# Gates by joined products, a fifth place for split weights at the second norm, and a first unit split by halves, in a two-block float32 kernel

## The chip, the core and the metric

The kernel runs on one core of a Trainium2 chip. The metric is the time of one execution on the device in microseconds (us); several executions are timed and their median is given. TensorE is called PE here (PEld for its weight loads), VectorE DVE, ScalarE ACT, GpSimd POOL and SyncE SP, as in the profile.

## The reference

Two residual blocks run one after the other over 256 tokens of width 1024 in float32. The first has a Mamba-2 mixer and an RG-LRU mixer, joined by gates, and a gated feed-forward block (FFN). The second has four branches, each gated and projected up, then summed and projected out:

```python
def _layer(x, mem, ...):
    h = _rmsnorm(x, norm_pre)
    cols = h @ w_in
    (dn_qkv, dn_z, dn_b, dn_a, gm_uv, gm_z, sw_q, sw_k, sw_v, sw_z,
     xm_q, xm_z, gate_logits) = _split_cols(cols)
    mem_kv = _rmsnorm(mem, norm_mem) @ w_mem_kv
    y_a = _deltanet_branch(dn_qkv, dn_z, ...)      # o * silu(z), z = dn_z
    y_b = _spatial_gating_branch(gm_uv, gm_z, ...)
    y_c = _sliding_window_branch(sw_q, sw_k, sw_v, sw_z, sinks)   # o * silu(z), z = sw_z
    y_m = _memory_branch(xm_q, xm_z, mem_kv)
    proj = jnp.einsum("btnc,ncd->btnd", ys, w_up)
    merged = jnp.sum(sigmoid(gate_logits) * proj, axis=2)
    return x + _rmsnorm(merged @ w_out, norm_post)
```

The change is about `sw_z` and `dn_z` (512 columns each), about the norms between the FFN and this block, and about the very first product.

## The kernel before

**Weights in units.** All weights come from one stream of 258 units of 128x1024 float32 (512 KB). SP fetches them in order into five buffers `t_raw`, each fetch behind the split of the unit five before it. A unit is split in two: ACT writes its high part to `t_wh` (fp32r), then DVE writes the rest, raw minus high, to `t_wl` (`split`, L1333 on ACT and L1903 on DVE). There are NS = 4 places for split units, so unit q's place is free when PE has finished unit q-4. PE waits for the low part before it starts a unit.

**Products.** Inputs are split too, into Hh and Hl, two halves of one tile `t_hx`. A product is high by high, high by low and low by high; low by low is left out. In `three` (L643 to L645) this takes three matmuls with 256 columns (tokens) for each 128 rows of weights; a unit has eight such k steps, a chunk of 256 output columns has two units, and its two halves lie in one PSUM bank. `chunk_apart` (L701), used by 19 of the 24 FFN chunks, joins the first two: one matmul of 512 columns multiplies the high weights by Hh and Hl together, and one of 256 adds the low weights by Hh to one half:

```python
mm(two(b), wh[:, k, :], HX[:, :, k, :], k == 0, False)
return mm(half(b, 1), wl[:, k, :], Hh[:, k, :], False, k == 7)
```

Each unit then fills a bank, and DVE adds the bank's halves with a TENSOR_REDUCE (L2613). `turned` (L728) makes rows of tokens: the inputs are stationary, the weights move in 512 columns, and token tiles tt = 0 and 1 go to two banks, six matmuls each per unit.

**Order.** Each engine's program is written out in one fixed order. A counter is advanced after each unit (`tick`, and `mid` inside a unit on PE) and at set counts lets the lanes go on: delta rule (`dn`), memory attention (`xm`), sliding attention (`sw`) and others. So an engine does unit work, then what its lanes have due, then the gate of the chunk, strictly in that order. Three banks, 0 to 2, go round among the chunks; who had a bank before (`bank_table`, L263, and `evacuated`, L532) must have been read before PE writes it again.

**Gates.** `swz0`, `swz1`, `dnz0`, `dnz1` are the last chunks before the gate logits `gt3_0`. Each is 2 units. When a chunk is done ACT takes tanh(z/2) from the bank (`half_tanh`, L1807), and DVE computes (tanh + 1) * z (`gated`, L2631) from the bank again.

**The second norm** (`second_norm`, L1389 on ACT, L2034 on DVE) stands between the FFN and the second block: squares of the FFN's output, its norm, the residual, the norm of the sum, the scaled rows; then PE transposes them (`turn_tile`, L772), tile by tile, and ACT and DVE take high and low parts. While it runs PE has four units of its own: `mk2` (two) and `mk3` (two), from the memory's normed rows, of which the last comes after the first transposes. After them `vu` (four units) needs the transposed rows. `walk.ahead(n)` inside the norm splits units up to n at set places among the norm's steps.

**The start.** ACT scales the input's high parts, then splits unit 0, takes squares and splits unit 1; DVE follows with the low parts. PE has the small product for dt, then `xbc4` with unit 0, in whose second unit it sums the squares (`mix_sums`); in `xbc5` it spreads the row of the norm over all partitions (`norm_spread`), and DVE and ACT make the normed inputs from that.

Of the kernel before, what the change touches and what calls it, by code (L numbers as in the profile page):

```python
# [202 lines left out]
class Walk:  # L203
# [5 lines left out]
    def unit(self, ahead=NS - 1):  # L209
        q = self.q  # L210
        self.q += 1
        while self.split_to <= min(q + ahead, NU - 1):
            self.split(self.split_to)
            self.split_to += 1
        return q

    def ahead(self, q):
        while self.split_to <= q:
            self.split(self.split_to)
            self.split_to += 1  # L220
# [124 lines left out]
def build_program(nc, first, gates, ws, par, con, masks, bd, rows, swt, xin, xtok, min_, post, decay, gates2, out):  # L345
    ctx = ExitStack()
    with ctx:
# [47 lines left out]
        s_raw = [sem(f"s_raw{i}") for i in range(NR)]  # L395
        HX = sb("hx", [P, 2, 8, T], R)
# [43 lines left out]
        FSUM = ar(32, 4, T)  # L440
        QKV = ar(0, 12, T)
# [90 lines left out]
        def evacuated(name):  # L532
# [106 lines left out]
        def pe_program(e):  # L639
# [13 lines left out]
            def weights(q, a):  # L653
                return [w[q % NS][:, :].rearrange("p (a b) -> p a b", a=a) for w in (WH, WL)]

            def split_ready(q):
                e.wait_ge(*lo.of(q))
# [507 lines left out]
            chunk("xbc4", YBh, YBl, {(1, 4): mix_sums})  # L1165
# [85 lines left out]
            for i in range(2):  # L1251
                for j in range(2):
# [47 lines left out]
            for name in ("swz0", "swz1", "dnz0", "dnz1"):  # L1300
                chunk(name, Hh, Hl)
# [30 lines left out]
        def act_program(e):  # L1332
            def split(q):  # L1333
                e.wait_ge(s_raw[q % NR], 16 * (q // NR + 1))
                if q >= NS:
                    e.wait_ge(*unit_done(q - NS))
                e.activation(WH[q % NS][:, :], RAW[q % NR][:, :], ACT.Copy, bias=0.0, scale=1.0).then_inc(*hi.now(q))  # L1337
# [51 lines left out]
            def second_norm(q):  # L1389
# [6 lines left out]
                walk.ahead(q + 1)  # L1396
# [22 lines left out]
                tile_parts(1, range(8))  # L1419
                act(BAS[:, :, 0:8], BAW, ACT.Copy).then_inc(*a_rw.now("w"))  # L1420
# [248 lines left out]
            split(0)  # L1669
# [106 lines left out]
            walk.four(3)  # L1776
# [30 lines left out]
            def half_tanh(name, dst):  # L1807
                for i in range(2):
                    walk.cols(f"{name}{i}")
                    chunk_done(f"{name}{i}")  # L1810
                    act(dst[:, 2 * i:2 * i + 2, :], two(BANK[f"{name}{i}"]), ACT.Tanh, scale=0.5).then_inc(*a_ev.now("tanh", f"{name}{i}"))
# [90 lines left out]
        def dve_program(e):  # L1902
            def split(q):  # L1903
                e.wait_ge(*hi.of(q))
                e.tensor_tensor(WL[q % NS][:, :], RAW[q % NR][:, :], WH[q % NS][:, :].bitcast(F), SUB).then_inc(*lo.now(q))  # L1905
# [128 lines left out]
            def second_norm(q):  # L2034
# [7 lines left out]
                walk.ahead(q + 1)  # L2042
# [6 lines left out]
                walk.ahead(q + 2)  # L2049
# [3 lines left out]
                walk.ahead(q + 3)  # L2053
                row_rsqrt(pre, 1, 1)
                scaled(pre, 1)
                walk.ahead(q + 4)
                tile_lows(0, range(6))
                walk.ahead(q + 5)
# [430 lines left out]
            split(0)  # L2489
# [128 lines left out]
            walk.four(3)  # L2618
            second_norm(FIRST["mk2"])
# [301 lines left out]
```

## Time and profile before

| | us |
|---|---|
| median of 3 runs | 853.13 (852.63 to 854.49) |
| the profiled execution: its own time | 853.44 |
| its span, first to last instruction | 851.6 |
| PE busy | 836.5 (98%), 5422 matmuls |
| DVE busy | 651.1 (76%) |
| ACT busy | 508.6 (60%) |
| POOL busy | 74.7 (9%) |
| DMA, share of 16 engines | 50.8% |

The share of busy time says how full an engine was. The timeline gives start and duration of each instruction, or of several alike merged (x2), and in brackets how long the engine was idle before it and which engine's instruction ended that. Matmul ends are modelled and overlap, so PE's pace is read from start to start.

### The profile page before, as it was taken

Reading aid. Unit: us, or ns where it says so; the run is one execution under the profiler, and the core shown is the slowest. Engines: PE = TensorE matmul, PEld = TensorE weight load, DVE = VectorE, ACT = ScalarE, POOL = GpSimd, SP = SyncE. Lnnn points to the kernel's source line nnn. Section 1 sums busy time; section 2 is a strip of 40 time slices with the busy share of each in tenths; the row PEclk is TensorE's granted clock in tenths of the full one; section 3 lists DMA queues with packets and bytes.
Section 4 is the critical chain, followed back from the end, with each engine's and each line's share of the span. In section 5 each row is a group of like instructions: output and inputs, shape, how many; then the busy total and the mean of one; then the engine's idle time right before and its main releaser. Section 6 shows DMA issues by size and latency. Waiting matters only on the chain. (4 is left out here: it accounts for less than half of the span.)

```text
span 851.6 us, 13942 instructions
## 1 busy us (share of the span) xinstructions
PE 836.5 (98%) x5422; PEld 754.9 (89%) x5422; DVE 651.1 (76%) x1169; ACT 508.6 (60%) x839; POOL 74.7 (9%) x76
## 2 busy tenths in 40 slices
PE   8999999999999999999999899999999999999996
PEld 6999999999989988888888699899899888888885
DVE  6887987998877877888777968788855476776765
ACT  6575778665377755565656878754554444545443
POOL 0100002001020211111111200140000020000000
PEclk9999999999999999999999999999999999999999
DMA  8657443467455655556555465644433332355641
GB/s 311 233 170 282 152 146 125 149 199 296 145 179 182 228 185 198 178 174 205 187 193 179 133 214 171 239 162 149 138 110 103 115 130 99 128 198 194 198 149 49
DMA packets 40585, 148.42 MB, mean 174 GB/s; under 512 B 4652, under 2 KB 5320, under 8 KB 39880
## 3 DMA queue, kind: packets, MB, share of 16 engines
q1 hardware_dynamic: 40520, 147.54, 50.8%
q8 instruction: 43, 0.70, 0.3%
q14 instruction: 22, 0.18, 0.1%
HBM read 146.44 MB, written 1.08 MB: 173 GB/s over the span
## 5 line engine op out<-in xcount | busy, mean ns | idle before, releaser
L1905 DVE TENSOR_TENSOR t_wl<-t_raw,t_wh 128x1024 fp32r<-128x1024 f32 x258 | 315.3, 1231 | 81.4 <-ACT t_wh L1337 80.0
L1337 ACT ACTIVATE t_wh<-t_raw 128x1024 fp32r<-128x1024 f32 x258 | 270.4, 1055 | 90.1 <-PE bank L648 49.9
L643 PE MATMUL bank<-t_hx,t_wh 128*128 128x256 f32 x832 | 241.9, 291 | 1.3 <-DVE t_wl L1905 1.2
L645 PE MATMUL bank<-t_hx,t_wl 128*128 128x256 f32 x832 | 235.4, 283 | 0.0
L644 PE MATMUL bank<-t_hx,t_wh 128*128 128x256 f32 x832 | 235.3, 283 | 0.0
L643 PEld LDWEIGHTS bank<-t_hx,t_wh 128*128 128x128 f32 x832 | 159.2, 191 | 4.0 <-DVE t_wl L1905 2.0
L644 PEld LDWEIGHTS bank<-t_hx,t_wh 128*128 128x128 f32 x832 | 159.2, 191 | 0.5
L645 PEld LDWEIGHTS bank<-t_hx,t_wl 128*128 128x128 f32 x832 | 159.1, 191 | 0.0
L648 PE MATMUL bank<-t_wh,t_hx 128*128 128x512 f32 x448 | 150.3, 401 | 3.2 <-DVE t_wl L1905 3.2
L648 PE MATMUL bank<-t_wh,t_br 128*128 128x512 f32 x384 | 123.5, 393 | 0.0
L648 PE MATMUL bank<-t_hx,t_wh 128*128 128x512 f32 x304 | 107.7, 398 | 0.0
L648 PEld LDWEIGHTS bank<-t_wh,t_hx 128*128 128x128 f32 x448 | 84.2, 188 | 20.9 <-DVE t_wl L1905 4.1
L648 PE MATMUL bank<-t_wl,t_hx 128*128 128x512 f32 x224 | 87.4, 390 | 0.0
L648 PEld LDWEIGHTS bank<-t_wh,t_br 128*128 128x128 f32 x384 | 72.1, 188 | 15.4 <-issue 0.2
L648 PE MATMUL bank<-t_hx,t_wl 128*128 128x256 f32 x304 | 85.3, 281 | 0.0
L648 PE MATMUL bank<-t_wl,t_br 128*128 128x512 f32 x192 | 74.9, 390 | 0.0
L1342 ACT ACTIVATE t_arena<-bank 128x512 f32<-128x512 f32 (+5 forms) x76 | 42.0, 573 | 54.4 <-PE bank L648 28.2
L648 PEld LDWEIGHTS bank<-t_hx,t_wh 128*128 128x128 f32 x304 | 57.1, 188 | 14.1
L2704 POOL TENSOR_TENSOR t_br<-t_arena,t_br 128x256 fp32r<-128x256 f32 x29 | 33.6, 1163 | 400.3 <-ACT t_br L1342 400.3
L648 PE MATMUL bank<-t_arena 128*128 128x128 f32 (+4 forms) x370 | 58.4, 305 | 1.2 <-DVE t_arena L2483 1.2
L648 PEld LDWEIGHTS bank<-t_hx,t_wl 128*128 128x128 f32 x304 | 57.4, 189 | 0.4
L1920 DVE SCALAR_TENSOR_TENSOR t_arena<-bank,t_par,t_arena 128x255 f32<-128x255 f32 (+3 forms) x108 | 43.9, 474 | 15.4 <-ACT t_arena L1342 15.0
(153 smaller groups left out, 984.4 us busy)
## 6 DMA issues: line engine op xcount, KB each, us to landing
t_raw<-in_ws SPq DMA_DIRECT2D x258, 512.0 KB, 4.0
t_br<-decay SPq DMA_DIRECT2D x1, 2048.0 KB, 8.8
t_arena<-in_post SPq DMA_DIRECT2D x3, 512.0 KB, 5.1
t_arena<-gates SPq DMA_DIRECT2D x1, 1536.0 KB, 10.4
t_x<-in_xin SPq DMA_DIRECT2D x2, 512.0 KB, 4.8
t_bd<-in_bd SPq DMA_DIRECT2D x1, 1024.0 KB, 7.5
t_x<-in_xtok SPq DMA_DIRECT2D x1, 1024.0 KB, 6.4
t_arena<-in_mem SPq DMA_DIRECT2D x1, 1024.0 KB, 8.5
```

The source lines that it names most:

```text
L643: e.matmul(o, wh, xh, start=first, stop=False, skip_group_check=True)
L644: e.matmul(o, wh, xl, start=False, stop=False, skip_group_check=True)
L645: return e.matmul(o, wl, xh, start=False, stop=last, skip_group_check=True)
L648: return e.matmul(o, l, r, start=st, stop=sp, skip_group_check=True)
L1337: e.activation(WH[q % NS][:, :], RAW[q % NR][:, :], ACT.Copy, bias=0.0, scale=1.0).then_inc(*hi.now(q))
L1342: return e.activation(o, i, f, bias=bias, scale=scale)
L1905: e.tensor_tensor(WL[q % NS][:, :], RAW[q % NR][:, :], WH[q % NS][:, :].bitcast(F), SUB).then_inc(*lo.now(q))
L1920: return e.scalar_tensor_tensor(out=o, in0=a, scalar=s, in1=b, op0=op0, op1=op1)
L2704: return e.tensor_tensor(o, a, b, op)
```

## The change

Four edits, with what goes with them:

1. `swz0`, `swz1`, `dnz0`, `dnz1` go through `chunk_apart`. Each unit has a bank of its own, DVE adds the halves of both banks to a new tile ZSUM (arena, float32), and tanh on ACT and the gate on DVE read ZSUM. The bank is free again at the event ("sum", chunk), when both units' halves are added.
2. The unit SPARE, the second of `mk2`, gets a place of its own in `t_br`, whose first half is idle there. It is split at the end of the FFN; inside the second norm `walk.ahead` passes over it, so each place where a unit was split now splits the one after it.
3. In `mk3`'s last unit PE does token tile 0, then `turn_tile(0)`, then token tile 1; before, `turn_tile(0)` came ahead of both.
4. Unit 0 is split in two halves of 512 columns on ACT and DVE, and PE waits for the second ahead of k step 4.

```diff
     def ahead(self, q):
         while self.split_to <= q:
-            self.split(self.split_to)
+            if self.split_to != SPARE:
+                self.split(self.split_to)
             self.split_to += 1
...
+SPARE = FIRST["mk2"] + 1
+def place(q):
+    return (q - (q > SPARE)) % NS
+def had_place(q):
+    if q == SPARE:
+        return LAST["fd9"]
+    return q - NS - (SPARE < q <= SPARE + NS)
+GATES_APART = ("swz0", "swz1", "dnz0", "dnz1")
...
+        elif name in GATES_APART:
+            for i in range(2):
+                n = (n + 1) % 3
+                bank[name, i] = n
...
             def split_ready(q):
-                e.wait_ge(*lo.of(q))
+                e.wait_ge(*(lo.of(q) if q else lo.of(0, "first")))
...
-            chunk("xbc4", YBh, YBl, {(1, 4): mix_sums})
+            chunk("xbc4", YBh, YBl, {(0, 4): lambda: e.wait_ge(*lo.of(0)), (1, 4): mix_sums})
...
-                    if i == 1 and j == 1:
-                        turn_tile(0)
                     for tt in range(2):
                         m = turned(f"mk{2 + i}", u, 4 * i + 2 * j, Hh, Hl, i == 0 and j == 0, i == 1 and j == 1, (tt,))
                         if i == 1 and j == 1 and tt == 0:
                             m.then_inc(*p_tok.now("mk3"))
+                            turn_tile(0)
...
-            for name in ("swz0", "swz1", "dnz0", "dnz1"):
-                chunk(name, Hh, Hl)
+            for name in GATES_APART:
+                chunk_apart(name)
...
+            def split_by_halves(q):
+                e.wait_ge(s_raw[q], 16)
+                for c in range(2):
+                    e.activation(WH[q][:, halves(c)], RAW[q][:, halves(c)], ACT.Copy, bias=0.0,
+                                 scale=1.0).then_inc(*(hi.now(q) if c else hi.now(q, "first")))
...
-                walk.ahead(q + 1)
+                walk.ahead(q + 2)
                 post_squares(post, 1, 0)
...
-                walk.ahead(q + 2)
+                walk.ahead(q + 3)
                 x_squares(post, pre, 1, 0)
                 x_squares(post, pre, 1, 1)
-                walk.ahead(q + 3)
+                walk.ahead(q + 4)
                 scaled(pre, 0)
                 root(pre, 1, 1)
-                walk.ahead(q + 4)
+                walk.ahead(q + 5)
                 scaled(pre, 1)
...
+                    if f"{name}{i}" in GATES_APART:
+                        e.wait_ge(*d_ev.of("sum", f"{name}{i}"))
+                        src = ZSUM
...
             def gated(name, dst):
+                if name in GATES_APART:
+                    at = GATES_APART.index(name)
+                    e.wait_ge(*(d_ev.of(GATES_APART[at - 1]) if at else d_gm.of("v", 1)))
+                    for i in range(2):
+                        e.wait_ge(*unit.of(FIRST[name] + i))
+                        m = e.tensor_reduce(ZSUM[:, i, :], two(BANK[name, i]).rearrange("p w t -> p t w"), AX.X, ADD)
+                    m.then_inc(*d_ev.now("sum", name))
                 e.wait_ge(*a_ev.of("tanh", name))
-                stt(dst, dst, 1.0, two(BANK[name]), ADD, MUL).then_inc(*d_ev.now(name))
+                stt(dst, dst, 1.0, ZSUM if name in GATES_APART else two(BANK[name]), ADD, MUL).then_inc(*d_ev.now(name))
```

**How it moves the order.** DVE at the end of `dnz1`, before: the split of a unit (TENSOR_TENSOR to `t_wl`), the maxima of the last memory-attention head (bank 7), its reciprocal and scaling (`t_px`), the gate of `dnz1` from bank 0, the next split.

```order
L1905 TENSOR_TENSOR t_wl0<-t_raw4,t_wh0 128x1024 [waits s_split_hi]
L2425 TENSOR_REDUCE t_sm<-bank7 128x1 [waits s_xm_pe]
L2425 TENSOR_REDUCE t_sm<-bank7 128x1
L1916 TENSOR_SCALAR t_sm<-t_sm 128x2 [waits s_xm_dve]
L2430 RECIPROCAL t_sm<-t_sm 128x2 [waits s_xm_act]
L1916 TENSOR_SCALAR t_px<-t_px,t_sm 128x256 [waits s_xm_dve]
L1916 TENSOR_SCALAR t_px<-t_px,t_sm 128x256
L1920 SCALAR_TENSOR_TENSOR t_arena<-t_arena,bank0 128x512 [waits s_evac_act]
L1905 TENSOR_TENSOR t_wl1<-t_raw0,t_wh1 128x1024 [waits s_split_hi]
```

The same place now, with `dnz1` in banks 0 and 1:

```order
L1951 TENSOR_TENSOR t_wl3<-t_raw4,t_wh3 128x1024 [waits s_split_hi]
L2477 TENSOR_REDUCE t_sm<-bank7 128x1 [waits s_xm_pe]
L2477 TENSOR_REDUCE t_sm<-bank7 128x1
L1968 TENSOR_SCALAR t_sm<-t_sm 128x2 [waits s_xm_dve]
L2482 RECIPROCAL t_sm<-t_sm 128x2 [waits s_xm_act]
L1968 TENSOR_SCALAR t_px<-t_px,t_sm 128x256 [waits s_xm_dve]
L1968 TENSOR_SCALAR t_px<-t_px,t_sm 128x256
L2690 TENSOR_REDUCE t_arena<-bank0 128x256 [waits s_unit,s_evac_dve]
L2690 TENSOR_REDUCE t_arena<-bank1 128x256 [waits s_unit]
L1972 SCALAR_TENSOR_TENSOR t_arena<-t_arena 128x512 [waits s_evac_act]
L1951 TENSOR_TENSOR t_wl0<-t_raw0,t_wh0 128x1024 [waits s_split_hi]
```

Two sums of halves have come in between the scaling and the gate, and the gate no longer reads a bank.

PE after `dnz1`, before: the scores of the last memory-attention head (bank 7), then the first unit of `gt3_0`, token tile 0 in bank 1 and token tile 1 in bank 2.

```order
L648 MATMUL bank7<-t_arena 128x256 [waits s_xm_dve]
L648 MATMUL bank7<-t_arena 128x256
L648 MATMUL bank1<-t_wh2,t_hx 128x512 [waits s_evac_dve,s_split_lo]
L648 MATMUL bank1<-t_wl2,t_hx 128x512
L648 MATMUL bank1<-t_wh2,t_hx 128x512 x2
L648 MATMUL bank1<-t_wl2,t_hx 128x512
L648 MATMUL bank1<-t_wh2,t_hx 128x512
L648 MATMUL bank2<-t_wh2,t_hx 128x512 [waits s_evac_dve]
L648 MATMUL bank2<-t_wl2,t_hx 128x512
L648 MATMUL bank2<-t_wh2,t_hx 128x512 x2
```

The same place now:

```order
L677 MATMUL bank7<-t_arena 128x256 [waits s_xm_dve]
L677 MATMUL bank7<-t_arena 128x256
L677 MATMUL bank2<-t_wh1,t_hx 128x512 [waits s_evac_dve,s_split_lo]
L677 MATMUL bank2<-t_wl1,t_hx 128x512
L677 MATMUL bank2<-t_wh1,t_hx 128x512 x2
L677 MATMUL bank2<-t_wl1,t_hx 128x512
L677 MATMUL bank2<-t_wh1,t_hx 128x512
L677 MATMUL bank0<-t_wh1,t_hx 128x512 [waits s_evac_dve]
L677 MATMUL bank0<-t_wl1,t_hx 128x512
L677 MATMUL bank0<-t_wh1,t_hx 128x512 x2
```

The tiles have moved to banks 2 and 0. Bank 0 was that of `dnz1`'s first unit, so the wait on `s_evac_dve` at the third row from the end is for the two sums above.

ACT in the second norm, before (`t_wh` rows are splits; `t_raw3` holds `mk2`'s second unit, `t_raw4` and `t_raw0` the two of `mk3`).

```order
L1342 ACTIVATE t_sm<-t_sm 128x1 [waits s_row_square,s_row_added]
L1337 ACTIVATE t_wh1<-t_raw3 128x1024 [waits s_unit,s_raw3]
L1363 ACTIVATE t_arena,t_sm<-bank6 128x512 [waits s_tokens_done]
L1363 ACTIVATE t_arena,t_sm<-t_x 128x512 [waits s_row_added]
L1363 ACTIVATE t_arena,t_sm<-bank7 128x512 [waits s_unit]
L1342 ACTIVATE t_sm<-t_sm 128x1 [waits s_row_square,s_row_added]
L1363 ACTIVATE t_arena,t_sm<-t_x 128x512 [waits s_row_added]
L1342 ACTIVATE t_sm<-t_sm 128x1 [waits s_row_square,s_row_added]
L1337 ACTIVATE t_wh2<-t_raw4 128x1024 [waits s_unit,s_raw4]
L1363 ACTIVATE t_arena,t_sm<-t_x 128x512 [waits s_row_added] x2
L1337 ACTIVATE t_wh3<-t_raw0 128x1024 [waits s_unit,s_raw0]
```

The same place now:

```order
L1376 ACTIVATE t_sm<-t_sm 128x1 [waits s_row_square,s_row_added]
L1365 ACTIVATE t_wh1<-t_raw4 128x1024 [waits s_unit,s_raw4]
L1397 ACTIVATE t_arena,t_sm<-bank6 128x512 [waits s_tokens_done]
L1397 ACTIVATE t_arena,t_sm<-t_x 128x512 [waits s_row_added]
L1397 ACTIVATE t_arena,t_sm<-bank7 128x512 [waits s_unit]
L1376 ACTIVATE t_sm<-t_sm 128x1 [waits s_row_square,s_row_added]
L1397 ACTIVATE t_arena,t_sm<-t_x 128x512 [waits s_row_added]
L1376 ACTIVATE t_sm<-t_sm 128x1 [waits s_row_square,s_row_added]
L1365 ACTIVATE t_wh2<-t_raw0 128x1024 [waits s_unit,s_raw0]
L1397 ACTIVATE t_arena,t_sm<-t_x 128x512 [waits s_row_added] x2
L1365 ACTIVATE t_wh3<-t_raw1 128x1024 [waits s_unit,s_raw1]
```

`t_raw3` is gone from the norm (it is split ahead of it, into `t_br`), and each split is of the unit after the one that stood there. DVE's order of splits moves in the same way.

## Rows read from the trace of the kernel before

**Rows 1.** Busy time by stretch: span, PE, PEld, DVE, ACT, POOL busy, PEclk, DMA share, GB/s
```profile
475.00:480.00 5.00, 3.01 (x12) 2.18 (x12) 4.89 (x12) 3.82 (x10) 0.00 (x0) 1.00 0.30 105
613.80:653.70 39.90, 39.80 (x332) 39.21 (x329) 22.84 (x34) 19.32 (x33) 0.00 (x0) 1.00 0.32 108
```

**Rows 2.** PE timeline, start: start us, us, instruction [idle before <-what ended it]
```profile
11.18 0.38 PE L643 MATMUL bank<-t_br,t_wh 128*128 128x256 f32 x1 [1.26 <-DVE t_wl L1905]
...
15.58 0.50 PE L648 MATMUL bank<-t_con,t_arena 128*128 128x1 f32 x4
```

**Rows 3.** PE timeline, second norm: mk2's second unit, mk3's first, turning, vu
```profile
475.50 0.50 PE L648 MATMUL bank<-t_wh,t_hx 128*128 128x512 f32 x1 [1.59 <-DVE t_wl L1905]
...
480.16 0.50 PE L648 MATMUL bank<-t_wh,t_hx 128*128 128x512 f32 x1 [1.65 <-DVE t_wl L1905]
...
483.05 1.04 PE L651 MATMUL bank<-t_con,t_arena 128*128 128x128 f32 x8
...
487.49 0.48 PE L648 MATMUL bank<-t_wh,t_hx 128*128 128x512 f32 x1
```

**Rows 4.** DVE timeline, start of the kernel
```profile
6.15 3.28 DVE L1920 SCALAR_TENSOR_TENSOR t_br<-t_x,t_arena,t_br 128x256 fp32r<-128x256 f32 x8 [2.92 <-ACT t_br L1342]
...
11.04 0.69 DVE L1910 TENSOR_TENSOR t_arena<-t_arena 128x512 f32<-128x512 f32 x1
...
13.03 1.94 DVE L1910 TENSOR_TENSOR t_arena<-t_arena 128x512 f32<-128x512 f32 x3
```

**Rows 5.** ACT timeline, start: split of unit 0; first normed input
```profile
8.82 1.04 ACT L1337 ACTIVATE t_wh<-t_raw 128x1024 fp32r<-128x1024 f32 x1
...
20.06 0.81 ACT L1342 ACTIVATE t_hx<-t_arena 128x256 fp32r<-128x256 f32 x2 [0.43 <-DVE t_arena L1920]
```

**Rows 6.** DVE timeline, second norm: three splits, then low parts of tile 0
```profile
469.46 1.23 DVE L1905 TENSOR_TENSOR t_wl<-t_raw,t_wh 128x1024 fp32r<-128x1024 f32 x1 [4.12 <-ACT t_wh L1337]
...
474.23 1.21 DVE L1905 TENSOR_TENSOR t_wl<-t_raw,t_wh 128x1024 fp32r<-128x1024 f32 x1
...
478.88 1.22 DVE L1905 TENSOR_TENSOR t_wl<-t_raw,t_wh 128x1024 fp32r<-128x1024 f32 x1
...
485.30 1.65 DVE L1920 SCALAR_TENSOR_TENSOR t_hx<-bank,t_par,t_hx 128x128 fp32r<-128x128 f32 x6 [0.32 <-ACT t_hx L1342]
```

**Rows 7.** ACT timeline, end of FFN, then scaled rows of either tile
```profile
464.46 0.42 ACT L1342 ACTIVATE t_br<-t_arena 128x256 fp32r<-128x256 f32 x1 [1.44 <-DVE t_arena L1910]
...
480.89 0.73 ACT L1342 ACTIVATE t_arena<-t_x,t_sm 128x512 f32<-128x512 f32 x1 [0.22 <-DVE t_sm L1917]
...
483.36 0.72 ACT L1342 ACTIVATE t_arena<-t_x,t_sm 128x512 f32<-128x512 f32 x1 [0.61 <-DVE t_sm L1917]
```

**Rows 8.** PE timeline, joined products, first and last of 32 k steps
```profile
398.28 0.39 PE L648 MATMUL bank<-t_hx,t_wh 128*128 128x512 f32 x1
...
409.57 0.40 PE L648 MATMUL bank<-t_wh,t_br 128*128 128x512 f32 x1
```

**Rows 9.** PE timeline, plain products of a chunk, 70 matmuls apart
```profile
562.80 0.28 PE L644 MATMUL bank<-t_hx,t_wh 128*128 128x256 f32 x1
...
571.20 0.28 PE L645 MATMUL bank<-t_hx,t_wl 128*128 128x256 f32 x1
```

**Rows 10.** DVE timeline, a pair of half sums in the FFN
```profile
443.81 1.28 DVE L2613 TENSOR_REDUCE t_arena<-bank 128x256 f32<-128x512 f32 x2
```

**Rows 11.** DVE timeline, the lane's last step and swz0's gate
```profile
627.34 1.01 DVE L1920 SCALAR_TENSOR_TENSOR t_arena<-t_arena,bank 128x256 f32<-128x256 f32 x2
```

**Rows 12.** ACT timeline, in swz1: the delta rule's bank is emptied
```profile
628.78 0.60 ACT L1342 ACTIVATE t_arena<-bank 128x512 f32<-128x512 f32 x1 [4.44 <-PE bank L648]
```

**Rows 13.** PE timeline: that bank's transposes; first matmul of gt3_0
```profile
630.82 0.60 PE L651 MATMUL bank<-t_con,t_arena 128*128 128x128 f32 x4
...
653.70 0.59 PE L648 MATMUL bank<-t_wh,t_hx 128*128 128x512 f32 x1
```

**Rows 14.** DVE timeline, end of dnz1: the gate, behind the memory lane's scaling
```profile
656.87 0.68 DVE L1920 SCALAR_TENSOR_TENSOR t_arena<-t_arena,bank 128x512 f32<-128x512 f32 x1
```

More of the change, by code:

```diff
@@ L211, in unit @@
         self.q += 1
[L212 to L214 removed]
+        self.ahead(min(q + ahead, NU - 1))
         return q
@@ L395, in build_program, with high, low @@
         s_raw = [sem(f"s_raw{i}") for i in range(NR)]
+        def high(q):
+            return BR[:, 0, 0:1024] if q == SPARE else WH[place(q)][:, :]
+        def low(q):
+            return BR[:, 1, 0:1024] if q == SPARE else WL[place(q)][:, :]
         HX = sb("hx", [P, 2, 8, T], R)
@@ L540, in evacuated @@
                     return d_ev.of(name[0])
+                if name[0] in GATES_APART:
+                    return d_ev.of("sum", name[0])
                 if name[0][:2] == "wo":
@@ L653, in weights @@
             def weights(q, a):
-                return [w[q % NS][:, :].rearrange("p (a b) -> p a b", a=a) for w in (WH, WL)]
+                return [w.rearrange("p (a b) -> p a b", a=a) for w in (high(q), low(q))]
             def split_ready(q):
-                e.wait_ge(*lo.of(q))
+                e.wait_ge(*(lo.of(q) if q else lo.of(0, "first")))
             def bank_free(name):
@@ L1335, in split @@
                 if q >= NS:
-                    e.wait_ge(*unit_done(q - NS))
-                e.activation(WH[q % NS][:, :], RAW[q % NR][:, :], ACT.Copy, bias=0.0, scale=1.0).then_inc(*hi.now(q))
+                    e.wait_ge(*unit_done(had_place(q)))
+                e.activation(high(q), RAW[q % NR][:, :], ACT.Copy, bias=0.0, scale=1.0).then_inc(*hi.now(q))
+            def split_by_halves(q):
[3 more added lines that the diff above has]
+                                 scale=1.0).then_inc(*(hi.now(q) if c else hi.now(q, "first")))
             walk = Walk(split)
@@ L1419, in second_norm @@
                 tile_parts(1, range(8))
+                e.wait_ge(*unit.of(SPARE))
                 act(BAS[:, :, 0:8], BAW, ACT.Copy).then_inc(*a_rw.now("w"))
@@ L1668, in act_program @@
                 act(YBh[:, k, :], X[:, k, :], ACT.Copy, scale=WMIX[:, k:k + 1]).then_inc(*a_xw.now(k))
-            split(0)
+            split_by_halves(0)
             for i in range(4):
@@ L1775, in act_program @@
                     walk.cols(f"fd{(j - 3) // 2}")
-            walk.four(3)
+            for j in range(4):
+                walk.unit(3 - j)
+            while walk.t < T_FU[23] + 1:
+                walk.tick()
+            split(SPARE)
+            while walk.t < T_FU[23] + 3:
+                walk.tick()
             chunk_done("fu23")
@@ L1809, in half_tanh @@
                     walk.cols(f"{name}{i}")
-                    chunk_done(f"{name}{i}")
-                    act(dst[:, 2 * i:2 * i + 2, :], two(BANK[f"{name}{i}"]), ACT.Tanh, scale=0.5).then_inc(*a_ev.now("tanh", f"{name}{i}"))
+                    if f"{name}{i}" in GATES_APART:
+                        e.wait_ge(*d_ev.of("sum", f"{name}{i}"))
+                        src = ZSUM
+                    else:
+                        chunk_done(f"{name}{i}")
+                        src = two(BANK[f"{name}{i}"])
+                    act(dst[:, 2 * i:2 * i + 2, :], src, ACT.Tanh, scale=0.5).then_inc(*a_ev.now("tanh", f"{name}{i}"))
             def rows_of_tokens(name, dst, f, event, scale=1.0):
@@ L1904, in split, with split_by_halves @@
                 e.wait_ge(*hi.of(q))
-                e.tensor_tensor(WL[q % NS][:, :], RAW[q % NR][:, :], WH[q % NS][:, :].bitcast(F), SUB).then_inc(*lo.now(q))
+                e.tensor_tensor(low(q), RAW[q % NR][:, :], high(q).bitcast(F), SUB).then_inc(*lo.now(q))
+            def split_by_halves(q):
+                for c in range(2):
+                    e.wait_ge(*(hi.of(q) if c else hi.of(q, "first")))
+                    e.tensor_tensor(WL[q][:, halves(c)], RAW[q][:, halves(c)], WH[q][:, halves(c)].bitcast(F),
+                                    SUB).then_inc(*(lo.now(q) if c else lo.now(q, "first")))
             walk = Walk(split)
@@ L2041, in second_norm @@
                 post_added(post, 0)
-                walk.ahead(q + 1)
+                walk.ahead(q + 2)
                 row_bias(post, 0, 1)
@@ L2048, in second_norm @@
                 post_added(post, 1)
-                walk.ahead(q + 2)
+                walk.ahead(q + 3)
                 row_rsqrt(pre, 1, 0)
@@ L2618, in dve_program @@
             walk.four(3)
+            split(SPARE)
             second_norm(FIRST["mk2"])
```

10 lines of the change are left out of this document (5 added, 5 removed).

## The prediction

> **What bounds the kernel now.** The table of busy time comes first: PE 98%, DVE 76%, ACT 60%, DMA 51% of the span. That is a mean over stages, so the windows are read next. In the 39.90 us that hold the four gates PE is busy for 39.80 and DVE for 22.84; in the 5 us around the second norm PE is busy for only 3.01 and DVE for 4.89 [rows 1]. So PE's stream sets the time, except where PE waits, and an edit is worth what it does to that stream. The brackets of PE's timeline give the waits that this change can touch, all ended by a low part from DVE: 1.26 us ahead of the first product [rows 2], 1.59 ahead of `mk2`'s second unit and 1.65 ahead of `mk3`'s first [rows 3]. They sum to 4.50 us; all else must come from PE doing less, or go by new waits.
>
> **Unit 0 by halves (edit 4).** ACT splits the whole unit from 8.82, for 1.04 [rows 5]; half of it is ready at about 9.39. DVE is held by the eight low parts of the input until 6.15 + 3.28 = 9.43, and a subtraction of 512 columns takes it 0.69 [rows 4]; so the first low half is there at about 10.15 and PE starts near 10.2, not 11.18: 1.0 earlier. It doesn't keep that. The sum of squares at 15.58 [rows 2] needs DVE's last additions, which end at 13.03 + 1.94 = 14.97 [rows 4], and some 0.1 later now, since two short splits cost more than a long one. So it comes near 15.1, and 0.48 is left. Then the norm's result releases ACT for the first normed input at 20.06, after an idle time of 0.43 [rows 5]: ACT is busy with splits until 19.63, so it can't begin before about 19.70. What is left is 0.36. **Term: −0.36**, ends 0 and −1.0.
>
> **The spare unit and the turning (edits 2 and 3).** Both waits of [rows 3] are for a split late in DVE's order [rows 6]. Now `mk2`'s second unit is split at the end of the FFN. ACT has 1.44 idle there [rows 7] for a split of 1.04, and DVE 4.12 [rows 6] for one of 1.2. So PE goes on without the wait of 1.59. The low part that ended at 474.23 + 1.21 = 475.44 [rows 6] is now that of `mk3`'s first unit, in time too; the one that ended at 478.88 + 1.22 = 480.10 is that of its second, and PE starts that unit at 480.16, where it started the first before. From there PE took 7.33 to `vu` (487.49 [rows 3]) for two units and two turnings. A unit is the 2.89 from 480.16 to the first turning at 483.05 [rows 3], a token tile 1.45 and a turning 0.78. Now: tile 0 to 481.61; the turning waits for ACT's scaled row, which ends at 480.89 + 0.73 = 481.62 [rows 7], and is done at 482.43; tile 1 to 483.88; the second turning waits for the scaled row that ends at 483.36 + 0.72 = 484.08 [rows 7] and is done near 484.95. `vu` needs its first two low parts: six take 1.65 from 485.30, a start that ACT's high parts set [rows 6], so two are there at 485.85, and `vu` starts near 485.95 instead of 487.49. Of the 3.24 removed, 1.70 comes back as three shorter waits. **Term: −1.54**. The ends are 0 (the order on ACT or DVE gives it all back) and −3.24.
>
> **Fewer matmuls in the gates (edit 1).** In the FFN 32 joined k steps take 409.57 − 398.28 = 11.29, or 0.3528 each [rows 8]. In a plain chunk 70 matmuls take 571.20 − 562.80 = 8.40, so 0.1200 each and 0.3600 a k step [rows 9]. The columns are the same 768, and only a fixed cost of one matmul falls away. Four chunks of 16 k steps: 64 × 0.0072 = 0.46. **Term: −0.46**. The Trainium skill, "TensorE: Matmul & The Clock Gate", section "Wait — 56ns, not 53.3ns?", has a fixed cost of about 2.5 ns a matmul beyond its columns at 2.4 GHz; by it 64 matmuls fewer give only 0.16, and the sum would end 0.30 higher. The trace's rows are used since they time these very forms.
>
> **The sums that this needs (edit 1).** DVE gains a pair of half sums per gate, 1.28 each time [rows 10], 5.1 in all. DVE has 17 us idle in that stretch [rows 1], so the work itself is covered; what isn't is work queued behind it, at two places.
>
> *At `swz0`.* The tanh on ACT used to wait for the product alone; now it waits for DVE, whose memory lane has a step before the gate ([rows 11]: two merged, the gate is the second, so the lane ends near 627.70). The sums end near 627.70 + 1.28 = 628.98, the tanh (0.6) near 629.5, then a split (1.04) near 630.5, and only then does ACT empty the delta rule's bank, which began at 628.78 after 4.44 idle before [rows 12]; it ends near 631.1. PE wants to transpose from it at 630.82 [rows 13], or some 0.1 earlier with joined products. **Term: +0.40**, ends 0 and +1.0. The next chunk's second unit wants the bank of the same sums near 629.1, which they just meet. At `swz1` and `dnz0` I take nothing, since DVE's idle time covers the shift; C below is the price if that cover is gone.
>
> *At the end of `dnz1`.* This is the largest term. `gt3_0` starts at 653.70 with token tile 0 [rows 13]. Its six matmuls take 1.45 as above, and 0.13 more behind the lane (the first lasts 0.59 here, 0.50 at 480.16), so tile 1 is due near 655.28. Its bank is now that of `dnz1`'s first unit, free when the sums are done. On DVE these stand behind the whole softmax of the last memory head. The gate followed the scaling at 656.87 [rows 14]; the sums take its place, and end at 656.87 + 1.28 = 658.15. The gate itself never held PE, since its bank wasn't wanted that soon. PE waits from 655.28 to about 658.25, that is 2.97, and its first matmuls after a wait cost 0.1 more, as at 475.50 (0.50, where the joined ones of [rows 8] last 0.39). Nothing behind gives it back: PE's stream simply goes on 3 us later. **Term: +3.07**. The ends are +2.0 (DVE reaches the softmax sooner) and +3.5 (the split and the maxima ahead of it shifted by 0.4).
>
> **Sum:** −0.36 − 1.54 − 0.46 + 0.40 + 3.07 = +1.11. The profiled execution took 853.44, which gives 854.55. It stood 0.31 above the median of the runs, so on the scale of that median it is 853.13 + 1.11 = **854.2**.
>
> **Rivals.**
> *A. The stall at `gt3_0` is absent or nearly so.* For it: DVE has 17 us idle in the stretch, and the softmax's wait for ACT may shrink. Against it: the order rows place both sums behind the scaling, without exception, and that scaling ends 1.6 us after the bank is wanted. Time: 853.13 + 1.11 − 3.07 = 851.2. Chance 0.15.
> *B. The second norm gives its gain back.* Its place is ACT and DVE at 463 to 486: if the spare's split finds its raw data or `t_br` late, ACT's high part of the last FFN input (464.46 [rows 7]) slips; DVE is nearly full there (4.89 of 5.00 [rows 1]). It decides once that slip is above the 1.54. Time: 854.2 + 1.54 = 855.8. Chance 0.11.
> *C. More of the order slips in the gates.* Tanh now waits for DVE four times, splits and bank emptying follow it on ACT. If PE waits at each of the three other gates as at `swz0`, or half a us each, it is +1.5: 855.7. Chance 0.08.
> *D. The clock falls in the wait of 3 us.* In [rows 1] the granted clock is 1.00, the 2.4 GHz level, through waits of 1.59 and 1.65. This one is almost twice as long, and no row here shows such a wait, or the 1.2 GHz level, in steady work. Bounds: nothing, as in those rows, and the wait's length again (3 us of products at half the clock take 6); taken in the middle, +1.5: 855.7. Chance 0.04. The Trainium skill, same page, section "HAM oscillation — how this bites in real kernels", describes such a fall of the clock after longer idle gaps of TensorE; where it applied, the time would be this rival's.
>
> **How the numbers follow.** The forecast has the remaining 0.62. A measurement of this kernel tells a change from none at about 0.2%, or 1.7 us: below 851.4 is faster, above 854.8 slower. The forecast is 0.6 below that upper bound, and its terms are loose by about 0.6 to one side (stall up to +3.5, `swz0` up to +1.0, the norm less than 1.54), so 0.45 of it falls within, 0.15 above and 0.02 below. A: two thirds of its 0.15 below 851.4. B, C and D (0.23) lie above but for 0.03. Together faster 0.12, same 0.53, slower 0.35. The forecast's own range is 853.3 to 855.2; the range of 8 in 10 reaches into A (851.6) and to B, C and D (856.2).
>
> **What the profile after would show.** PE's first product near 10.2, but the first normed input near 19.7. No PE wait at `mk2`'s second unit, about a us at `mk3`'s second, and short ones at the turnings and `vu`, which starts 1.5 earlier against the FFN's end. Gates with k steps of 0.353. In `gt3_0` a PE wait of about 3 us, ended by a TENSOR_REDUCE of DVE. The forecast is wrong if that wait is under 2 us, if the gates' k steps stay at 0.360, if `vu` doesn't start earlier against the FFN's end, or if PE waits over 1 us anywhere between `swz0` and `dnz1`.

## The result, and the profile after

The changed kernel takes 855.52 us in the median (12 executions, 853.79 to 855.74), against 853.13: a ratio of 1.0017 (95% interval 1.0009 to 1.0025), or 1.4 us slower. The two medians lie 2.4 apart, more than the ratio says, because the times fall into two groups, and the median before lies in the lower one, the median after in the upper one. The median is inside the predicted range of 8 in 10 (851.6 to 856.2) and 1.3 above the point of 854.2, but outside the forecast's own range (853.3 to 855.2): it lies in the part that was there for the rivals B, C and D. The profiled execution took 855.68, its span is 853.8. It stands against 853.44 and 851.6 before, so the two traces differ by 2.2 us.

The times of both kernels fall into these groups, some 1.5 us apart. Before: 8 of 12 in 852.63 to 853.57, 4 in 854.28 to 854.49. After: 4 of 12 in 853.79 to 854.13, 8 in 855.14 to 855.74. The lower groups differ by about 1.0, close to the forecast's +1.11, and the rest of the shift is that more executions are in the upper group. The mean granted clock of each execution goes with its group: 0.998 in all four of the changed kernel's lower group, 0.996 or 0.997 in its eight upper ones. What makes the groups is therefore half of this case.

From the page of the kernel after:

```profile
span 853.8 us, 13832 instructions
...
PE 839.0 (98%) x5358; PEld 753.9 (88%) x5358; DVE 655.1 (77%) x1178; ACT 509.0 (60%) x840; POOL 75.2 (9%) x76
```

64 matmuls fewer, as written (5422 before), and 4.0 us more for DVE. Who PE waited for, kernel after (us in total, times, longest), the rows that are new:

```profile
PE bank L677 <- DVE t_arena L2690: 2.8, 1, 2.8
...
PE bank L677 <- DVE t_wl L1951: 0.8, 1, 0.8
...
PE bank L677 <- issue: 0.6, 1, 0.6
...
PE bank L680 <- ACT t_arena L1376: 0.2, 1, 0.2
```

The two waits of 1.6 [rows 3] and the one of 1.26 [rows 2] are gone. The largest is now one of 2.8 for L2690, the sums of halves. PE's timeline shows the places. At the start:

```profile
10.12 0.58 PE L672 MATMUL bank<-t_br,t_wh 128*128 128x256 f32 x1
...
15.12 0.58 PE L677 MATMUL bank<-t_con,t_arena 128*128 128x1 f32 x4 [0.19 <-DVE t_arena L1962]
...
27.47 0.39 PE L672 MATMUL bank<-t_hx,t_wh 128*128 128x256 f32 x1 [0.44 <-DVE t_wl L1951]
```

PE starts 1.06 earlier (10.12 for 11.18), waits at the sum of squares (15.12 for 15.58), and is 0.39 ahead at a product of the normed input (27.47; that row stood at 27.86 before). That product, the one behind a short wait for DVE, is called the mark below: later stages are measured from it. Second norm, kernel after:

```profile
473.36 2.88 PE L677 MATMUL bank<-t_br,t_hx 128*128 128x512 f32 x12
...
479.76 0.50 PE L677 MATMUL bank<-t_wh,t_hx 128*128 128x512 f32 x1 [0.80 <-DVE t_wl L1951]
...
481.28 1.09 PE L680 MATMUL bank<-t_con,t_arena 128*128 128x128 f32 x8
...
483.75 1.09 PE L680 MATMUL bank<-t_con,t_arena 128*128 128x128 f32 x8
...
485.46 0.47 PE L677 MATMUL bank<-t_wh,t_hx 128*128 128x512 f32 x1 [0.63 <-issue]
```

`mk2`'s second unit (weights from `t_br`) follows without a wait, the low part of `mk3`'s second unit comes after 0.80, and `vu` starts at 485.46. Measured from the mark, that is 457.99 for 459.63: 1.64 earlier.

The gates, then `gt3_0`, kernel after:

```profile
628.55 0.66 PE L680 MATMUL bank<-t_con,t_arena 128*128 128x128 f32 x4 [0.18 <-ACT t_arena L1376]
...
631.72 0.39 PE L677 MATMUL bank<-t_hx,t_wh 128*128 128x512 f32 x1
...
632.42 0.40 PE L677 MATMUL bank<-t_hx,t_wh 128*128 128x512 f32 x1
...
651.20 0.58 PE L677 MATMUL bank<-t_wh,t_hx 128*128 128x512 f32 x1
...
655.71 0.76 PE L677 MATMUL bank<-t_wh,t_hx 128*128 128x512 f32 x1 [2.76 <-DVE t_arena L2690]
656.26 0.63 PE L677 MATMUL bank<-t_wl,t_hx 128*128 128x512 f32 x1
...
658.40 1.44 PE L677 MATMUL bank<-t_arena 128*128 128x128 f32 x8
659.67 0.82 PE L677 MATMUL bank<-t_pw,t_arena 128*128 128x256 f32 x4
660.25 0.48 PE L677 MATMUL bank<-t_wh,t_hx 128*128 128x512 f32 x1
```

Two k steps take 632.42 − 631.72 = 0.70, so 0.35 each. The forecast's wait behind ACT at `swz0` is the first row. `gt3_0` starts 2.50 earlier than before (651.20 for 653.70); tile 1 of its first unit starts 4.51 later, where it took 1.58 before: 2.93 for the wait. DVE in that stretch:

```profile
651.59 0.76 DVE L2477 TENSOR_REDUCE t_sm<-bank 128x1 f32<-128x256 f32 x2
...
653.64 0.17 DVE L2482 RECIPROCAL t_sm<-t_sm 128x2 f32<-128x2 f32 x1 [1.09 <-ACT t_px L1656]
653.84 0.62 DVE L1968 TENSOR_SCALAR t_px<-t_px,t_sm 128x256 f32<-128x256 f32 x2
654.37 1.28 DVE L2690 TENSOR_REDUCE t_arena<-bank 128x256 f32<-128x512 f32 x2
```

The softmax first, with 1.09 of idling for ACT inside it, then the sums, which release PE. But the trace has one thing more. Behind the wait the matmuls of 512 columns start 0.43 apart, not 0.23 (656.26 and 656.69 are two such starts). Windows of the kernel after (columns as in rows 1):

```profile
655.00:656.00 1.00, 0.29 (x1) 0.29 (x2) 0.65 (x2) 0.31 (x1) 0.00 (x0) 0.89 0.00 0
656.00:657.00 1.00, 1.00 (x3) 0.81 (x3) 0.65 (x1) 1.00 (x2) 0.00 (x0) 0.50 0.00 0
...
658.00:659.00 1.00, 1.00 (x5) 0.91 (x4) 0.52 (x1) 0.00 (x0) 0.00 (x0) 0.50 0.00 0
...
660.00:661.00 1.00, 1.00 (x7) 0.87 (x6) 0.41 (x1) 0.47 (x1) 0.00 (x0) 1.00 0.98 393
```

The granted clock is 0.50 of full speed, the 1.2 GHz level, from shortly before 656 to after 659, right behind PE's wait. From tile 1's start to the next unit it takes 4.54 (655.71 to 660.25), where it took 2.84 before (655.28 to 658.12).

The sum over the two traces, stage by stage: start −0.39, second norm −1.64, `vu` to the gates −0.34, gates −0.13, the wait +2.93, the slow clock behind it +1.70, from there to the end +0.07; together +2.20, the difference of the spans. The term of −0.34 was not forecast: before, PE waited 0.18 at 556.02 for DVE, and started again slowly; with PE's work earlier against DVE's that wait falls away in this trace.

### The profile page after: what moved, and what is told of

Same layout as the page of the kernel before. It is cut to its first block and busy times, and to the rows that moved or that the text cites. A ratio compares the mean times of both kernels' runs of the same rounds, so it can differ in the third digit from the quotient of the medians.

```text
span 853.8 us, 13832 instructions
## 1 busy us (share of the span) xinstructions
PE 839.0 (98%) x5358; PEld 753.9 (88%) x5358; DVE 655.1 (77%) x1178; ACT 509.0 (60%) x840; POOL 75.2 (9%) x76
## 5 line engine op out<-in xcount | busy, mean ns | idle before, releaser
L672 PE MATMUL bank<-t_hx,t_wh 128*128 128x256 f32 x768 | 222.2, 289 | 1.3 <-DVE t_wl L1951 1.2
L673 PE MATMUL bank<-t_hx,t_wh 128*128 128x256 f32 x768 | 217.2, 283 | 0.0
L672 PEld LDWEIGHTS bank<-t_hx,t_wh 128*128 128x128 f32 x768 | 147.1, 192 | 3.9 <-DVE t_wl L1951 2.0
L673 PEld LDWEIGHTS bank<-t_hx,t_wh 128*128 128x128 f32 x768 | 147.2, 192 | 0.4
L677 PE MATMUL bank<-t_hx,t_wh 128*128 128x512 f32 x368 | 132.5, 402 | 0.0
L677 PEld LDWEIGHTS bank<-t_hx,t_wh 128*128 128x128 f32 x368 | 69.2, 188 | 16.3
L1376 ACT ACTIVATE t_arena<-bank 128x512 f32<-128x512 f32 (+5 forms) x72 | 39.8, 571 | 50.3 <-PE bank L677 26.0
L677 PEld LDWEIGHTS bank<-t_arena 128*128 128x128 f32 (+2 forms) x370 | 49.7, 191 | 6.8 <-DVE t_arena L2535 1.2
```

Source lines behind the costliest of these rows:

```text
L672: e.matmul(o, wh, xh, start=first, stop=False, skip_group_check=True)
L673: e.matmul(o, wh, xl, start=False, stop=False, skip_group_check=True)
L677: return e.matmul(o, l, r, start=st, stop=sp, skip_group_check=True)
L1376: return e.activation(o, i, f, bias=bias, scale=scale)
```

## The experiments

The theory at this point: the wait in `gt3_0` is due to the place of `dnz1`'s sums in DVE's order; the upper groups are executions in which a wait lets the clock fall, in the kernel before one of the second norm's. Twelve runs follow; two of them repeat the kernels before and after.

**early_sums.** DVE adds `dnz1`'s halves ahead of the last unit's split and tick (EARLY holds `dnz1`):

```diff
+                if name in EARLY:
+                    walk.unit()
+                    walk.tick()
+                    half_sums(name)
+                    walk.unit()
+                    walk.tick()
+                else:
+                    walk.cols(name)
```

> The changed kernel with one thing moved: DVE adds the halves of dnz1 before the last unit's split and the memory head's softmax, not behind them. Order theory (PE's wait of 2.76 in gt3_0 is for the place of these sums in DVE's order): the sums end near 651.6, before PE wants the bank at 652.8, the wait is under 0.2 and the granted clock stays 1.00 in 655 to 660; the time is 2.5 below that of before, near 850.5. Rival (the wait is for something else in the joined gates, or the softmax now comes late instead and PE waits there): a wait of over 1 us stays between 650 and 670 and the time is within 1 us of the changed kernel's lower runs, near 854.

Measured: 850.93 median (8 of 9 runs in 850.66 to 851.36, one at 852.97), ratio to before 0.9972 (0.9962 to 0.9981). DVE's timeline of this kernel:

```profile
650.12 1.28 DVE L2691 TENSOR_REDUCE t_arena<-bank 128x256 f32<-128x512 f32 x2
651.32 1.21 DVE L1951 TENSOR_TENSOR t_wl<-t_raw,t_wh 128x1024 fp32r<-128x1024 f32 x1
652.45 0.74 DVE L2477 TENSOR_REDUCE t_sm<-bank 128x1 f32<-128x256 f32 x2
```

And PE's, where the merged row holds tile 0's last matmul and tile 1's first:

```profile
652.28 0.62 PE L677 MATMUL bank<-t_wh,t_hx 128*128 128x512 f32 x2
652.74 0.39 PE L677 MATMUL bank<-t_wl,t_hx 128*128 128x512 f32 x1
```

(The rest of the edit moves the two sums out of `gated` into `half_sums`.) The sums end at 651.40, PE goes from tile 0 to tile 1 without a gap, and the softmax, now 1.1 later against PE's first product of `gt3_0`, holds up nobody. The order theory holds, and the interval of this version lies below 1, that of the changed kernel above. The one run at 852.97 is not explained.

**filled.** 12 matmuls into the idle bank 6 right ahead of the wait:

```diff
+                    if name == "gt3_0_0" and first and tt == 1:
+                        e.wait_ge(*a_sw.of("pt", *SW_ORDER[0]))
+                        for n in range(12):
+                            mm(PB[6][:, :], xh[:, k0, 0:128], wh[:, 0, :], n == 0, False)
```

> The changed kernel with 12 matmuls of 512 columns (2.73 us) put into the idle bank 6 right ahead of PE's wait in gt3_0; nothing reads them. Clock theory (the wait of 2.76 lets the clock fall, which costs 1.6 in the executions in which it happens): the next unit starts at the same time as in the changed kernel, but the granted clock stays 1.00 after it; all runs lie near 854.0, the lower level of the changed kernel, none near 855.6. Rival (the two levels of the changed kernel are a matter of the execution and not of this wait): two levels 1.6 apart stay, 854.0 and 855.6, or all moves up by the 2.7 of the added matmuls, to 857.

Measured: 853.95 median, 10 of 11 runs in 853.69 to 854.35, one at 856.99; ratio 1.0005 (0.9995 to 1.0015). PE's timeline of this kernel:

```profile
651.33 0.58 PE L677 MATMUL bank<-t_wh,t_hx 128*128 128x512 f32 x1
...
652.67 3.65 PE L677 MATMUL bank<-t_wh,t_hx 128*128 128x512 f32 x14
...
658.78 0.47 PE L677 MATMUL bank<-t_wh,t_hx 128*128 128x512 f32 x1
```

Its window (columns as in rows 1):

```profile
651.00:662.00 11.00, 10.96 (x58) 9.12 (x57) 5.95 (x12) 4.36 (x11) 0.00 (x0) 1.00 0.28 95
```

The second unit starts 7.45 behind the first, where it took 9.05 in the changed kernel and 4.42 before. So the delay of some 3 is all there, and 1.60 has gone with the fall of the clock: useless work is 1.6 us faster than a wait behind which the clock falls, and as fast as one behind which it doesn't (the changed kernel's lower group). The upper group is gone too, but for the run at 856.99, which was not profiled. The clock theory is right as to this wait.

**gates_alone.** Edit 1 alone (edits 2, 3 and 4 undone).

> The kernel before with edit 1 alone (joined gates). Sum theory: -0.45 for the columns, +0.1 at swz0, +2.9 for the wait in gt3_0, so +2.5 in the lower runs (near 855.4), and 1.6 more (near 857.0) in those in which the clock falls after it. Rival (the wait only shows because PE comes 2 us earlier to DVE in the changed kernel): the wait is under 1.5 here and the time near 853.5.

Measured: 857.24 to 857.52 in four runs and 859.52 in the fifth, the profiled one; ratio 1.0049 (1.0036 to 1.0063). PE's timeline of this kernel:

```profile
659.60 0.50 PE L677 MATMUL bank<-t_wh,t_hx 128*128 128x512 f32 x1 [2.76 <-DVE t_arena L2688]
```

Two of its windows:

```profile
660.00:662.00 2.00, 2.00 (x9) 1.68 (x8) 1.50 (x2) 1.16 (x2) 0.00 (x0) 0.66 0.00 0
662.00:664.00 2.00, 2.00 (x9) 1.82 (x8) 0.41 (x1) 0.60 (x1) 0.00 (x0) 0.50 0.31 82
```

The wait is 2.76 again, though PE is not 2 us ahead here: the rival is out. No run was near 855.4; all are at the level with the fall (852.9 − 0.13 + 2.93 + 1.6 = 857.3). The 859.52 needs a second fall, which this trace has at the start: its clock is 0.79 in 12 to 20, and its mark is at 29.73, not 27.86.

**no_gates.** Edits 2, 3 and 4 without edit 1.

> The changed kernel with plain gates (edits 2, 3 and 4 alone). Sum theory: -0.4 at the start and -1.6 at the second norm, so near 851.0, with no wait of over 1 us behind 30 us. As to the two levels of the kernel before (852.9 and 854.4): if its upper level is a fall of the clock behind the two waits of 1.6 in the second norm, there is one level here, near 851.0; if it is a matter of the execution, there are two, 851.0 and 852.5. Rival (the norm's gain is only moved): the PE timeline gets it back before dnq5, and the time is within 0.5 of before.

Measured: 850.91 median, six runs in 850.75 to 851.08, ratio 0.9967 (0.9955 to 0.9979). One group, as expected, though for a reason that the next runs overturn. The joined gates' own worth is read from here as well: from the lane's matmuls ahead of `swz0` to the start of `gt3_0` it takes 41.03 plain (610.29 to 651.32) and 40.93 in the changed kernel. They gain 0.1 there, and the kernel is 4.6 slower with them.

**halves_alone** and **norm_alone.** Edit 4 alone; edits 2 and 3 alone.

> The kernel before with edit 4 alone (unit 0 by halves). Sum theory: -0.3 to -0.4, so lower runs near 852.5. The two waits of 1.6 in the second norm are still there: if they are what lets the clock fall in some runs, there are two levels as in before, near 852.5 and 854.1. Rival (the edit is worth the whole 1.0 by which PE starts earlier): lower runs near 851.9.

> The kernel before with edits 2 and 3 alone (the spare unit, the turning moved). Sum theory: -1.6, so near 851.3, and one level, since no wait over 1 us is left behind 15 us. Rival (the levels are a matter of the execution): two levels, 851.3 and 852.8.

Measured: halves_alone 852.64, eleven runs of eleven in 852.43 to 853.03, one group; ratio 0.9991 (0.9982 to 1.0000). norm_alone 851.01 to 851.60 in six runs and 852.83 to 853.85 in five; ratio 0.9984 (0.9975 to 0.9993). Both sizes are as in the sum, and both groupings are the opposite of what was expected: the kernel that keeps the two waits of 1.6 has one group, the one that removes them has two. The theory of the second norm has fallen. What halves_alone removes is the wait ahead of the first product, so the groups must come from the start.

**before_again.** The kernel before, once more.

> The kernel before once more, for its profile. If the profiled execution is of the upper level (854.4 or more), the granted clock theory says that its clock is below 1.00 behind one of the two waits of 1.6 us, between 475 and 490 us, and that vu starts some 1.5 later against the FFN than in the lower level. Rival: the clock is 1.00 there and the time went elsewhere (the first fetches, the end).

Measured: 855.39, span 853.6, as long as the upper group or longer. PE waits 1.58 and 1.60 in the second norm and its clock is 1.00 there. But windows at the start of this execution show:

```profile
8.00:10.00 2.00, 2.00 (x11) 0.71 (x10) 1.54 (x4) 2.00 (x5) 0.00 (x0) 0.72 1.05 418
10.00:12.00 2.00, 0.97 (x5) 0.71 (x4) 1.83 (x3) 2.00 (x4) 0.00 (x0) 0.50 1.02 417
12.00:14.00 2.00, 2.00 (x11) 2.00 (x10) 1.90 (x3) 1.95 (x3) 0.00 (x0) 0.50 1.03 399
14.00:16.00 2.00, 2.00 (x13) 2.00 (x12) 1.97 (x3) 0.00 (x0) 0.00 (x0) 0.57 0.98 318
```

PE's timeline of the same execution:

```profile
11.29 0.58 PE L643 MATMUL bank<-t_br,t_wh 128*128 128x256 f32 x1 [1.03 <-DVE t_wl L1905]
...
29.92 0.39 PE L643 MATMUL bank<-t_hx,t_wh 128*128 128x256 f32 x1 [0.45 <-DVE t_wl L1905]
```

The clock is at 0.50, its 1.2 GHz level, from 10 to 14. The first product starts 0.11 later than before (11.29), the mark comes at 29.92 instead of 27.86; from there to the end both executions take the same (823.68 and 823.74). So the 2.0 us by which this execution is longer are lost in its first 16 us. The fall begins near 8.9, ahead of the wait of 1.03.

**spare_alone** and **turn_alone.** Edit 2 alone; edit 3 alone.

> The kernel before with edit 2 alone (the spare unit; the turning of tile 0 stays ahead of both token tiles). The first turning then waits for the scaled row of 481.6 with nothing before it, so mk3's second unit starts 0.6 later than with edit 3 and vu near 486.1 instead of 487.49: -1.4, where both edits gave -1.6. Rival (edit 3 is what matters): vu starts at 487 or later.

> The kernel before with edit 3 alone (the turning of tile 0 behind token tile 0). Both waits of 1.6 stay, and vu starts 7.3 behind the second of them, as in before: worth 0. Rival (the edit shortens a wait by itself): vu starts 0.3 or more earlier.

Measured, one run each: 853.33 and 855.57. PE's timeline of spare_alone:

```profile
481.69 1.94 PE L680 MATMUL bank<-t_con,t_arena 128*128 128x128 f32 x8 [2.46 <-ACT t_sm L1380]
...
487.72 0.48 PE L677 MATMUL bank<-t_wh,t_hx 128*128 128x512 f32 x1
```

A window of it:

```profile
480.00:485.00 5.00, 3.31 (x12) 3.05 (x13) 4.64 (x13) 4.17 (x10) 0.00 (x0) 0.66 0.59 189
```

The first turning starts when expected, but PE has by then waited 2.46, the clock falls, and `vu` starts at 487.72, 460.01 behind the mark: 0.4 later than before, not 1.4 earlier. From the turning to `vu` it takes 6.03 here and took 4.44 before [rows 3] for the same work, so 1.59 of it is the slow clock; without the fall `vu` would come some 1.2 earlier than before (an estimate from these two). PE's timeline of turn_alone:

```profile
490.78 0.50 PE L677 MATMUL bank<-t_wh,t_hx 128*128 128x512 f32 x1 [0.38 <-DVE t_wl L1952]
...
492.68 0.50 PE L677 MATMUL bank<-t_wh,t_hx 128*128 128x512 f32 x1 [0.23 <-DVE t_wl L1952]
```

Both waits of 1.60 stay, `vu` starts at 488.77, 459.52 behind the mark (0.1 earlier), and then two new waits come in `vu`, since tile 0's parts and the splits behind them are a token tile later. In these single executions each edit alone is worth nothing or less, edit 2 because of the fall; together they are worth 1.64. In the pair, token tile 0's products stand where spare_alone waits for the turning, and no wait there is over 0.8. The long total of turn_alone is again the start: its clock was 0.93 in 12 to 30, and its mark is at 29.25.

**early_swz0_plain** (early sums, `swz0` plain) and **dnz1_plain** (`dnz1` plain, the other sums as in the change).

> The changed kernel with dnz1's sums early and swz0 plain again, so that tanh of swz0 no longer waits for DVE. Order theory (the joined gates lose 0.33 of their 0.46 at swz0, where PE waits 0.2 for a bank that ACT empties late and starts again slowly): no wait of PE between 615 and 650, swz0 to gt3_0 takes 40.7 (40.93 with all four joined and dnz1's sums early, 41.06 plain), and the time is 0.2 below that of dnz1's sums early alone, near 850.7. Rival (the loss is in the columns, not at swz0): it takes 40.9 or more.

> The changed kernel with dnz1 plain and the other three gates joined, the sums where the change put them. The bank theory (PE waits in gt3_0 because tile 1's bank is dnz1's, freed by its late sums): gt3_0's banks are now dnz0's, freed long before; no wait over 0.3 there, clock 1.00 in 655 to 660, one level of times near 850.9. Rival (any gate ahead of gt3_0 leads to a wait): a wait of over 1 us is left.

Measured: 850.89 (850.36 to 851.09; ratio 0.9966, 0.9954 to 0.9979) and 851.01 (850.83 to 851.24; ratio 0.9970, 0.9959 to 0.9981), no wait over 0.2 in the gates or in `gt3_0` in either, one group each. With `swz0` plain the wait for ACT's bank is gone and the gates take 40.61 (610.75 to 651.36), better than expected. The total doesn't show it: the wait for DVE of the kernel before at 556.02 is back in this trace (0.16, at 554.10), with its slow restart. dnz1_plain settles the bank: with `gt3_0`'s banks from `dnz0` there is no wait.

**after_again.** The changed kernel once more.

> The changed kernel once more, for its profile. If it is of the lower level (853.8 to 854.1), the clock theory says that the wait of 2.8 in gt3_0 is there, but the granted clock behind it is 1.00; if of the upper one (855.1 to 855.7), the clock is 0.5 for some 3.5 us behind it, as in the first profile.

Measured: 855.50, again the upper group: the wait is 2.76, and the clock is 0.50 in 657 to 659. An execution of its lower group was never caught in a profile.

**The start in all fourteen profiles.** In every profile PE is idle for the first 1.21. What differs are its waits between 5 and 12 us and the clock; the kernels marked H have unit 0 by halves:

| profile | PE's waits | clock at 0.50 | mark |
|---|---|---|---|
| norm_alone | 1.84, 0.92 | 7.6 to 11.0 | 28.03 |
| filled (H) | 1.80 | 7.4 to 10.9 | 27.59 |
| no_gates (H) | 1.66 | 7.5 to 11.0 | 27.50 |
| gates_alone | 0.74, 0.50, 1.55 | 12.1 to 15.5 | 29.73 |
| turn_alone | 1.49, 1.27 | 11.2 to 14.6 | 29.25 |
| before_again | 1.17, 1.03 | 8.9 to 15.7 | 29.92 |
| before, spare_alone | longest 1.26 and 0.80 | never | 27.86, 27.71 |
| the six others (H) | longest 0.56 to 1.06 | never | 27.21 to 27.65 |

PE's timeline of no_gates, an execution of 851.08 in a kernel of one group, then its first 12 us as a window, with the mean clock below 1.00:

```profile
6.72 3.45 PE L677 MATMUL bank<-t_br,t_wh 128*32 128x256 f32 x16 [1.66 <-DVE t_br L1975]
```

```profile
0.00:12.00 12.00, 9.13 (x38) 6.14 (x39) 5.98 (x15) 8.25 (x17) 0.20 (x4) 0.86 0.82 283
```

So halves don't keep the clock up: it falls in two of eight profiles with them. What a fall costs is another matter: falls that end by 11.0 cost some 0.3 at most; the three that last beyond 14 cost 1.4 to 2.1. The first long wait, for the input's low parts from DVE, was 0.56 to 1.84 with the same program there, so it differs from execution to execution, and the clock fell in all five profiles in which a wait of the start was 1.49 or longer, and in one of the nine in which none was.

## Why the prediction was right, and where not

- *The start, −0.36:* measured −0.39 in the trace and −0.3 in the group of halves_alone against the lower group before. The path through the sum of squares was the right one: PE starts 1.06 earlier and keeps 0.39. What the step missed is the edit's larger effect: the upper group of the kernel before (25 of the 65 executions that were timed here lie above 854) is gone. Of 39 runs with halves and without a long wait later (halves_alone, no_gates, early_sums, early_swz0_plain, dnz1_plain), all but one lie within 1 us of their kernel's fastest. In the profile shown before the clock was 1.00 at the start, so that trace could not tell. That a fall of the clock between 8.9 and 15.7 makes the difference is shown in three profiles; how halves avoid it is only argued. They cut the wait ahead of the first product (0.80 to 1.55 without them, 0.30 at most with them), behind which the falls of gates_alone and turn_alone begin, but that of before_again begins ahead of it.
- *The second norm, −1.54:* measured −1.64; `vu` started a little sooner than the low parts' row gave. Rival B is out.
- *Columns, −0.46, and swz0, +0.40:* k steps of 0.35 as forecast; together −0.13 for −0.06. With `swz0` plain the stretch takes 40.61 against 41.03, so 0.42 for three gates of four, where the rows' 0.46 for four gives 0.35: the term was, if anything, low. The Trainium skill, "TensorE: Matmul & The Clock Gate", section "Wait — 56ns, not 53.3ns?", gives an estimate of only 0.16 for all four, and the measurement decides against it.
- *Bank of gt3_0, +3.07:* measured +2.93. The mechanism, the releaser (a TENSOR_REDUCE of DVE) and the size were right; early_sums and dnz1_plain show the cause.
- *The step that failed* is "Nothing behind gives it back: PE's stream simply goes on 3 us later", with rival D, the fall of the clock, at 0.04 and +1.5. It came true in both profiles of the changed kernel, and its size was right: 1.60 to 1.70. By the groups it happened in 8 of the 12 executions. The forecast's +1.11 is what the other 4 show (+1.0). That the median fell within the stated range is therefore partly luck: it is there by a rival that had been given 0.04, where the sum alone ends at 854.2. I had let two waits of 1.6 that kept the clock speak for one of 3, and the clock of 1.00 in one trace for all executions. The Trainium skill, "TensorE: Matmul & The Clock Gate", section "HAM oscillation — how this bites in real kernels", ties such a fall to idle gaps longer than these; here waits of 2.76 and 2.46 were followed by one in all four traces that have them.
- *The stage between `vu` and the gates, −0.34,* wasn't looked at. A wait of 0.2 that goes or comes with small shifts is worth 0.3 here.

What stays open: why the clock stayed up in some executions of the changed kernel, since none of those was profiled; why the two waits of 1.6 in the second norm never brought it down, while waits of about that length in the start did; and why it fell in before_again, whose waits there (1.17 and 1.03) were no longer than those of the profile before (1.00 and 1.26).

## What to carry to other kernels

Where one engine is the bound, price a new wait on it by its length and, if it is much longer than the waits that the trace has, by a slow stretch behind it as well: here a wait of 2.8 us cost 4.6, of which 2.9 was delay and 1.7 the slow clock. Ask of each bank that changes hands which instruction now frees it and what stands ahead of that on its engine: moving two sums ahead of a softmax that nobody waited for gave 4.6 us back between the medians, and 3.0 against the executions in which the clock stayed up. And if the times of a kernel fall into groups, compare group with group, and profile until each group has been seen.

## What the runs showed of the hardware

- Behind waits of 2.76 (three traces) and 2.46 us (one) the granted clock went to 0.50, the 1.2 GHz level, for some 3 to 4 us; that cost 1.6 to 1.7 us. The fall did not always come with the first matmul: in gates_alone the first four still started at full pace, and it came 1.0 behind the wait.
- Behind two waits of 1.6 us, 3 us apart, it stayed at 1.00 in all five traces that have them (before, before_again, halves_alone, turn_alone, gates_alone).
- At the start, in the first 16 us, it went to 0.50 in six of fourteen profiles: in all five with a wait of 1.49 to 1.84 us there, and in one with waits of 1.17 and 1.03, which another profile of the same kernel (1.00 and 1.26) had without a fall. It cost 1.4 to 2.1 us where it lasted into the products behind 14 us, and 0.3 at most where it ended by 11.
- PE kept busy with matmuls whose result nobody reads kept its clock at 1.00 (filled), and the kernel's median was 1.6 us below that with the plain wait (853.95 for 855.52).
